# Four quadrants of TensorE in a chunked recurrence, and an attention product moved one stage earlier

## What is computed

```
merged = sigmoid(g_attn) * (attn @ w_branch_attn) + sigmoid(g_ssm) * (ssm @ w_branch_ssm)
x = x + merged @ w_out
```

```
def step(s, inp):
    r_t, w_t, k_t, v_t, a_t, b_t = inp
    sa = jnp.einsum('bhvk,bhk->bhv', s, a_t)
    s = s * w_t[:, :, None, :] + sa[..., :, None] * b_t[:, :, None, :] + v_t[..., :, None] * k_t[:, :, None, :]
    return s, jnp.einsum('bhvk,bhk->bhv', s, r_t)
```

## Time and profile before

| | us |
|---|---|
| median of three runs | 3174.82 |
| the profiled execution, its own time | 3175.19 |
| its span, first to last instruction | 3173.4 |
| the state space stage, 471 to 592 us of the span | 121 |
| merge, 630 to 946 us | 316 |
| the chunk recurrence's body, 1604 to 2163 us | 559 |

### The profile page before, as it was taken

The page is one execution under the profiler, slowest core; times in us unless marked ns, Lnnn a source line. Parts: engine busy times, 40 slices in busy tenths (PEclk is TensorE's granted clock), DMA queues, the critical chain, the costliest instruction groups (busy, mean ns, idle before and its releaser), DMA issues. The chain is left out here.

```text
span 3173.4 us, 62863 instructions
## 1 busy us (share of the span) xinstructions
PE 2646.6 (83%) x26974; PEld 2124.9 (67%) x26974; DVE 1730.7 (55%) x2178; ACT 945.1 (30%) x1392; POOL 638.7 (20%) x618
## 2 busy tenths in 40 slices
PE   4798985689989379997879999995495489999993
PEld 1586644456657368885279999993275478888882
DVE  2791549411114422664645555555533679999993
ACT  2121431200003310001323222321102057777772
POOL 0221458021100023220064434430000011001000
PEclk8899997889999689997589999997695579999997
DMA  9231003111113211110411111001325069999994
GB/s 372 68 142 66 1 15 104 45 43 40 53 36 130 91 53 60 47 41 11 159 36 24 24 24 24 17 11 44 139 93 207 0 265 403 399 399 395 394 388 148
DMA packets 128123, 397.55 MB, mean 125 GB/s; under 512 B 54570, under 2 KB 64426, under 8 KB 98066
## 3 DMA queue, kind: packets, MB, share of 16 engines
q1 hardware_dynamic: 116948, 355.32, 29.9%
q0 software_dynamic: 4608, 16.78, 2.2%
q10 hardware_dynamic: 6336, 21.99, 1.8%
HBM read 342.64 MB, written 51.42 MB: 124 GB/s over the span
## 5 line engine op out<-in xcount | busy, mean ns | idle before, releaser
L2832 DVE TENSOR_TENSOR ex_wl<-ew_raw,ex_wh 128x2048 fp32r<-128x2048 f32 x192 | 435.6, 2290 | 42.0 <-ACT ex_wh L2794 38.5
L2794 ACT ACTIVATE ex_wh<-ew_raw 128x2048 fp32r<-128x2048 f32 x192 | 367.5, 1919 | 216.1 <-PEq L89 109.3
L125 PE MATMUL sp_acc<-b2h_hi,sp_wh 128*128 128x512 f32 (+1 forms) x528 | 194.5, 368 | 12.0 <-POOL sp_wl L1534 12.0
L125 PE MATMUL sp_acc<-b2h_lo,sp_wh 128*128 128x512 f32 (+1 forms) x528 | 194.4, 368 | 0.0
L125 PE MATMUL sp_acc<-b2h_hi,sp_wl 128*128 128x512 f32 (+1 forms) x528 | 194.1, 368 | 0.0
L1022 DVE TENSOR_TENSOR merge_sg<-merge_acc,merge_sg 128x512 f32<-128x512 f32 x32 | 20.6, 686 | 264.3 <-ACT merge_sg L1008 264.3
L2073 ACT ACTIVATE rc_xt<-rc_ps 128x256 f32<-128x256 f32 x160 | 61.3, 383 | 243.9 <-PE rc_ps L2214 243.9
L2214 PE MATMUL rc_ps<-rc_x,rc_lm 64*64 64x64 f32 x3200 | 129.5, 219 | 2.3 <-DVE rc_x L2147 1.3
L2715 POOL DMA_INDIRECT x<-ex_o,ex_at x16 | 26.5, 1655 | 490.9 <-DVE ex_o L2855 490.9
L125 PE MATMUL merge_acc<-merge_hh,merge_wh 128*128 128x512 f32 x256 | 101.7, 397 | 24.9 <-DVE merge_hl L1015 19.5
L2703 POOL DMA_INDIRECT ex_xs<-h,ex_at x16 | 27.5, 1719 | 457.3 <-DVE ex_at L2857 434.4
(11 more groups left out here) (453 smaller groups left out, 6936.3 us busy)
## 6 DMA issues: line engine op xcount, KB each, us to landing
ew_raw<-in_exp_gate SPq DMA_DIRECT2D x64, 1024.0 KB, 7.2
ew_raw<-in_exp_up SPq DMA_DIRECT2D x64, 1024.0 KB, 9.2
ew_raw<-in_exp_down SPq DMA_DIRECT2D x64, 1024.0 KB, 7.8
b_pj<-in_ada_w SPq DMA_DIRECT2D x24, 1024.0 KB, 18.9
rc_ac<-ac SPq DMA_DIRECT2D x40, 256.0 KB, 3.7
merge_w<-in_w_merge SPq DMA_DIRECT2D x16, 512.0 KB
ac<-rp_ac SPq DMA_DIRECT2D x4, 2048.0 KB, 7.2
pr_w<-in_w_main SPq DMA_DIRECT2D x14, 512.0 KB
```

Of the source, the lines that this page charges most:

```text
L125: ins = nc.tensor.matmul(out, w[a][:, k, :], h[b][:, k, cols], start=(first and n == 0), stop=(last and n == 2))
L2794: nc.scalar.activation(wh[:, n % RING], raw[:, n % RING], ACT.Copy).then_inc(q["w_hi"], 1)
L2832: V.tensor_tensor(wl[:, n % RING], raw[:, n % RING], wh[:, n % RING].bitcast(f32), ALU.subtract).then_inc(q["w_lo"], 1)
```

## The change

Three edits. (1) In the recurrence both directions share PSUM: `ps[n]` has two banks, and the bank is chosen by the rows of the array that a product uses. `crossing` issues four products at a time, one for each quadrant, two of each direction; a head's result may then lie on the other half of the partitions (heads are paired, `paired`), since transposes now take whole 128 x 128 blocks (two heads of both halves; `turned`) and move a matrix to the other half as well. Products that must stay on their half (`staying`: with the state `S`, and the inverse) use two quadrants as before, into a bank chosen by direction. The parts of `right_side`, `outputs` that use the state are separate blocks, evacuated separately (`gs`, and a second addition to `y`); `solved` then has two terms. VectorE no longer makes the first transposed start value: it is transposed by TensorE and copied by ScalarE like at the other levels. One semaphore for both directions is waited for where there were two. The order of the steps is somewhat changed. (2) In `s5`, 16 units of the attention product (8 blocks x 2 halves, four k each) stand between the other work of TensorE; ScalarE copies each (`pF`, one bank) and stores it to DRAM (`branch`). `inputs` is cut into halves of one bank. (3) `merge` loads `branch` back into `merged` ahead of everything else, issues the state space product alone, and weighs the attention branch from `merged`.

State space stage (new parts):

```diff
-        pU = ph.ps("pU", [P, 2, 512])
+        pU = ph.ps("pU", [P, 512])
+        pF = ph.ps("pF", [P, 512])
+        out = pj[:, 6, :].rearrange("p (s n) -> p s n", s=2)
+        wb = pj[:, 7, :].rearrange("p (s k n) -> p s k n", s=2, k=4)
 # scalar
+                def branches(*units):
+                    for u in units:
+                        act.wait_ge(q["b_summed"], u + 1)
+                        if u >= 2:
+                            act.wait_ge(stored[u % 2], 16 * (u // 2))
+                        nc.scalar.activation(out[:, u % 2], pF[:], ACT.Copy).then_inc(q["b_ready"], 1)
+                        act.wait_ge(q["b_ready"], u + 1)
+                        act.dma_start(branch[u // 2, :, (u % 2) * 512:(u % 2 + 1) * 512], out[:, u % 2]).then_inc(stored[u % 2], 16)
 # tensor
+                def branches(*units):
+                    for u in units:
+                        b, h = u // 2, u % 2
+                        if h == 0:
+                            pe.wait_ge(b_loaded[b % 2], 16 * (b // 2) + 16)
+                        if u:
+                            pe.wait_ge(q["b_ready"], u)
+                        for k in range(4):
+                            last = nc.tensor.matmul(pF[:], wb[:, b % 2, k, :], pj[:, PJ_ZA + k, h * 512:(h + 1) * 512], start=(k == 0), stop=(k == 3))
+                        last.then_inc(q["b_summed"], 1)
 # tensor, order
-                inputs(0)
+                inputs(0, 0)
+                inputs(0, 1)
                 chunk_sums(0)
-                inputs(1)
+                inputs(1, 0)
+                branches(0)
+                inputs(1, 1)
+                branches(1)
                 chunk_sums(1)
-                for a in range(PASSES):
+                branches(2, 3)
+                for a in range(2):
                     outputs(a)
-                    if a + 2 < PASSES:
-                        inputs(a + 2)
+                    inputs(a + 2, 0)
+                    branches(4 * a + 4)
+                    inputs(a + 2, 1)
                     back(a)
-                    if a + 2 < PASSES:
-                        chunk_sums(a + 2)
+                    chunk_sums(a + 2)
+                    branches(4 * a + 5, 4 * a + 6, 4 * a + 7)
+                outputs(2)
+                back(2)
+                branches(12, 13, 14, 15)
+                outputs(3)
+                back(3)
```

Merge:

```diff
             def _(sp):
+                for b in range(KD):
+                    sp.dma_start(merged[:, b, :], branch[b]).then_inc(a_loaded, 16)
                 with sp.Fori(0, KD) as b:
...
-                        for r, first in enumerate((PJ_ZA, PJ_ZS)):
-                            for k in range(4):
-                                last = nc.tensor.matmul(acc[:, 4 * h + 2 + r, :], wb[:, 4 * r + k, :], pj[:, first + k, hs], start=(k == 0), stop=(k == 3))
+                        for k in range(4):
+                            last = nc.tensor.matmul(acc[:, 4 * h + 2, :], wb[:, k, :], pj[:, PJ_ZS + k, hs], start=(k == 0), stop=(k == 3))
...
+                dve.wait_ge(a_loaded, 16 * KD)
                 dve.sem_inc(done, 2)
...
-                        for r in range(2):
-                            nc.vector.tensor_tensor(sg[:, h, r, :], acc[:, 4 * h + 2 + r, :], sg[:, h, r, :], ALU.mult).then_inc(weighed, 1)
+                        nc.vector.tensor_tensor(sg[:, h, 0:1, :], merged[:, ds(b, 1), h * 512:(h + 1) * 512], sg[:, h, 0:1, :], ALU.mult).then_inc(weighed, 1)
+                        nc.vector.tensor_tensor(sg[:, h, 1, :], acc[:, 4 * h + 2, :], sg[:, h, 1, :], ALU.mult).then_inc(weighed, 1)
```

Recurrence, TensorE's new helpers and body (waits left out where a line of dots stands):

```diff
+        ps = [ph.ps(f"ps{n}", [P, 2, 512]) for n in range(4)]
-            b["ps"] = [ph.ps(f"ps{d}{i}", [P, 512]) for i in range(4)]
+        def crossed(n, d, w=CK):
+            return ps[n][:, :, d * 2 * w:(d + 1) * 2 * w].rearrange("p f (j t) -> p j f t", t=w)
+        def stayed(n, d, half=0):
+            return ps[n][:, d, half * HP * CK:(half + 1) * HP * CK].rearrange("p (h t) -> p h t", t=CK)
-                def heads(out, l, r, start=True, stop=True):
-                    for e in range(2):
-                        c = slice(e * CK, (e + 1) * CK)
-                        last = M(out[c], l[c], r[c], start=start, stop=stop)
+                def crossing(n, w, *terms):
+                    for j, s in product(range(HP // 2), range(2)):
+                        for i, (l, r) in enumerate(terms):
+                            for d, c in product(range(2), range(2)):
+                                f = c ^ s ^ d
+                                k, h, at = slice(f * CK, (f + 1) * CK), 2 * j + c, (2 * d + j) * w
+                                last = M(ps[n][c * CK:(c + 1) * CK, f, at:at + w], l(t[d])[k, h], r(t[d])[k, h], start=(i == 0), stop=(i == len(terms) - 1))
+                def staying(n, half, l, r):
+                    for h, d, c in product(range(HP), range(2), range(2)):
+                        k = slice(c * CK, (c + 1) * CK)
+                        last = M(stayed(n, d, half)[k, h], l(t[d])[k, h], r(t[d])[k, h], start=True, stop=True)
+                def turned(out, m):
+                    for j in range(HP // 2):
+                        pair = slice(2 * j, 2 * j + 2)
+                        last = nc.tensor.transpose(out[:, pair].rearrange("p h t -> p (h t)"), m[:, pair].rearrange("p h t -> p (h t)"), T.ident[:])
...
+                def body(i, sl, old, following):
                     products(i, 0, sl)
                     if old is not None:
                         right_side(i, 1 - sl)
+                    x_turned(i, 0, sl)
+                    crossing(3, 2 * CK, (lambda b: b["kst"][:, sl], lambda b: b["ar"][:, sl])).then_inc(joint["pk_done"], 1)
+                    if old is not None:
+                        right_side_of_state(i, 1 - sl)
                     advanced(i, 0, sl)
                     products(i, 1, sl)
+                    x_turned(i, 1, sl)
                     if old is not None:
                         solved(i, 1 - sl)
                     advanced(i, 1, sl)
...
+                            last = turned(stayed(3, d, half_), b[n][:, sl])
...
                     products(i, 2, sl)
+                    x_turned(i, 2, sl)
                     if old == "all":
                         outputs(i, 1 - sl)
                     advanced(i, 2, sl)
+                    if old == "all":
+                        outputs_of_state(i - CTX_CK, 1 - sl)
+                    products(i, 3, sl)
+                    x_turned(i, 3, sl)
                     if old is not None:
+                        state(i, 1 - sl)
+                    advanced(i, 3, sl)
+                    products(i, 4, sl)
+                    x_turned(i, 4, sl)
                     if following:
...
                         lower(i + 1, 1 - sl)
...
+                    for d in range(2):
+                        turned(stayed(3, d), t[d]["vst"]).then_inc(q[d]["v_done"], 1)
+                    advanced(i, 4, sl)
                     if following:
                         lower_rows(i + 1, 1 - sl)
-                    advanced(i, 4, sl)
```

More of the change, by code:

```diff
@@ L672, in _, with s5 @@
                         gate(it - 3)
-def s5(nc, T, uc, I, yT, work, rot, kept):
+def s5(nc, T, uc, I, yT, pj, rot, kept, branch):
     DG = 2 * GP
@@ L731, in _, with weights @@
                         sp.dma_start(wi[s * GC:(s + 1) * GC, :, :, :], kept.taps[a, :, :, CT - 1 - s:2 * CT - 1 - s, :]).then_inc(q["c_loaded"], 16)
+                def weights(b):
+                    if b >= 2:
+                        sp.wait_ge(q["b_summed"], 2 * b - 2)
+                    sp.dma_start(wb[:, b % 2], I["w_merge"][b, :, 2 * KD:2 * KD + 4]).then_inc(b_loaded[b % 2], 16)
+                sums(0)
+                weights(0)
+                weights(1)
+                outputs(0)
+                sums(1)
+                weights(2)
+                sums(2)
+                weights(3)
+                outputs(1)
+                sums(3)
+                weights(4)
+                weights(5)
+                outputs(2)
+                weights(6)
+                weights(7)
+                outputs(3)
             @block.gpsimd
@@ L1914, in rwkv_chunks @@
                 b[n] = ph.sb(f"{n}{d}", [P, 2, HP, CK])
-            for n in ("e_neg", "tmp", "t1", "vst", "v", "g", "u", "sum", "S"):
+            for n in ("e_neg", "tmp", "t1", "vst", "v", "g", "gs", "u", "sum", "S"):
                 b[n] = ph.sb(f"{n}{d}", [P, HP, CK])
@@ L2113, in masked @@
                         b, s = t[d], q[d]
-                        dve.wait_ge(s["t1_done"], LEVELS * i + l + 1)
-                        V.tensor_tensor(b["t1"][:], small(b["ps"][0]), over(T.level[d][l + 1][:]), ALU.mult).then_inc(s["t1_ready"], 1)
+                        dve.wait_ge(joint["t1_done"], LEVELS * i + l + 1)
+                        V.tensor_tensor(paired(b["t1"][:]), crossed(0, d), over(T.level[d][l + 1][:]), ALU.mult).then_inc(s["t1_ready"], 1)
```

(28 more changed lines are left out.)

295 lines of the change are left out of this document (131 added, 164 removed).

## The result

| | before | after |
|---|---|---|
| median of the runs | 3174.9 us | 3128.02 us (3126.26 to 3131.54) |
| ratio, 95% interval | | 0.9856 (0.9839 to 0.9873) |
| profiled execution: span | 3173.4 us | 3127.7 us |

The changed kernel is 47 us faster. I had forecast 139 us, and 3128 lies outside my range (2995 to 3100). The sign was right, the size was not.

The account below looks back on a forecast made before the run. Recurrence and merge were taken as bound by TensorE's stream of products, the state space stage not. 3175.2 - 105 (recurrence) - 48.5 (merge) + 14 (state space) = 3036 us; range 2995 to 3100.

Parts of the forecast that it names:

- the stage is explained by slots alone: Recurrence before the change: record slots sum to 27.8 us per full chunk, against 559 / 20 = 28.0.
- The sum for the changed chunk, 22.3 us: Recurrence: 17.2 us of TensorE work plus 4.6 idle, 21.5 in the first five chunks, plus 0.5 allowance.
- 0.5 for all of it: Recurrence: 0.5 us added per chunk for operations running beside GpSimd and for waits on two semaphores.
- bare schedule of 21.8: Recurrence: full chunk of 17.2 us TensorE work and 4.6 us idle, before the 0.5 allowance.
- The unknown prices: Recurrence: VectorE reading two banks, taken as nothing (possibly +40 us); four operands per slot instead of two, no row available.
- A: Recurrence: quadrants share no slot beyond pairs; 304 slots added, +9.6 us per chunk, stage +80, total 3221; chance 0.07.
- B: Recurrence: least spacing of 25 ns for every record, +5.7 us per chunk, stage 568, total 3150; chance 0.10.
- C: Recurrence: the clock falls, half the stage at 1.2 GHz, +8.6 us per chunk, total 3208; chance 0.04.
- the new stalls are at most 1.8 us: Recurrence, under the clock rival: TensorE's new idle pauses last no longer than 1.8 us each.
- 416 x 0.058 + 32 x 0.109: Recurrence before: narrow and wide pairs of a full chunk times their slot lengths, given as 27.8 us.
- forecast +3.5: Merge: branch loads queued ahead of the first weights delay TensorE's start by 3 to 5 us, taken as +3.5.
- The wait on `done`: Merge: state space half products end before the sum does, costing 0.4 us seven times, +3 in all.

Follow-up runs that it names:

- warm: The changed kernel with 96 more records (three crossings into a bank nobody reads) in TensorE's pause before each chunk: 3134.25 us, ratio 0.9866.
- two_at_a_time: The changed kernel with a crossing's outermost loop over s and f = c ^ s, 16 records in a row on the same two quadrants: 3177.16 us.
- late_turn: The changed kernel with GpSimd's factors held until x's start value, and x's transpose blocks replaced by crossings with the identity: 3176.94 us, ratio 1.0003.
- two_quadrants: The changed kernel with the loop over directions outermost in a crossing, the alternation of f kept: 3127.77 us, ratio 0.9846.

## Why the prediction was right and wrong

**The step that failed** is the claim that "the stage is explained by slots alone", carried over to a stage whose slots are half as long. It was true of the kernel before. The sum for the changed chunk, 22.3 us, has TensorE's slots and its waits for VectorE, and no term for how fast instructions arrive. Measured: 27.5. Of the 5.2 us missing, the stalls are 2.3. The additions beside GpSimd are 0.8 (2 x 0.83 less 2 x 0.42); I had seen that GpSimd lengthens VectorE's operations and put 0.5 for all of it. That 0.5 is already in the 22.3, so against the bare schedule of 21.8 the gap is 5.7. The half clock behind the longer pause is 1 to 1.5, which is an estimate: 0.45 for the transposes, 0.9 for the wide block and some for the block ahead, in most chunks; the run warm, at a clock of 1.00, is 1.6 us shorter outside its stalls. Between half a microsecond and one remains, which I leave open.

**The slots themselves were right.** Taking for every block the shortest time that it and the pause behind it have in 13 chunks, the sum for a chunk of the changed kernel is 23.2 us, or 22.4 without the 0.8 of the slow additions; my schedule says 21.8, and 22.3 with the allowance. A crossing takes 0.47 us, transposes 0.58 to the next block, the pauses behind levels 0 and 3 are 0.95 and 0.98 (forecast 1.16 and 1.31). Once GpSimd is out of the way, the pause ahead of a chunk is 1.62 us where 1.83 was forecast.

**The unknown prices.** Reading two banks costs VectorE nothing: 419 ns. Four operands instead of two per slot cost nothing: 32 records in 0.69 us.

**The rivals.** A is refuted by that row, and the quadrants' worth is shown by two_at_a_time: 29.4 us less stalls against 25.2. B, a least spacing of 25 ns for every record, is refuted too: records of a crossing start 14.6 ns apart. C was half right. The clock did fall, to 0.93, but not by half of the stage, and it cost 1 to 1.5 us per chunk where I had priced 8.6. It also needed a cause that I had excluded ("the new stalls are at most 1.8 us"). My own sign of being wrong, a clock below 0.95 in the recurrence, came. No rival had the instruction supply. The chance should have gone there, since the profile of before had the row: 92 instruction loads in 366 us, one per 4 us, for an engine whose records I was about to issue at twice the pace inside the crossings.

Three slips in the sums change nothing in this account: 416 x 0.058 + 32 x 0.109 is 27.6, not 27.8; rival A's 9.6 us goes with 272 slots, not 304; and its +80 leaves out the tail of 8 us, with which A would be some 7 us later.

**State space and merge.** The outputs of the four passes were forecast at 508.5, 539.2, 568.3 and 594.6 us; the stage began 1.4 us later than before, and they start as follows:

```profile
509.71 1.19 PE L890 MATMUL s_pB<-s_wi,s_um 128*128 128x128 f32 x4 [6.41 <-DVE s_x L964]
...
540.96 0.61 PE L890 MATMUL s_pB<-s_wi,s_um 128*128 128x128 f32 x4
...
569.69 0.61 PE L890 MATMUL s_pB<-s_wi,s_um 128*128 128x128 f32 x4
...
595.37 0.61 PE L890 MATMUL s_pB<-s_wi,s_um 128*128 128x128 f32 x4
```

That part holds step by step, the 3.43 us of a unit and the 1.1 us for its copy included. In merge TensorE starts 18.8 us into the stage where it was 16.1 before: +2.7 (forecast +3.5), and the row names the split weights as I had it:

```profile
664.50 0.79 PE L125 MATMUL merge_acc<-merge_hh,merge_wh 128*128 128x512 f32 x1 [21.69 <-POOL merge_wl L119]
```

The branch loads' starts lie 29.7 us apart (695.62, 725.32), before 36.6 (685.63, 722.25): 6.9 less, the full eight records twice over. The wait on `done`, for which I had set 0.4 us seven times, costs nothing. With the 0.8 us of the earlier start this is 3.8 of the 4.5 us by which merge was better.

## What to carry to other kernels

Instruction supply is a limit like any other: before and after an edit, work out how long the densest run of 256 instructions lasts. The mean over a stretch is not enough: before, 64 instructions per us lost next to nothing, and after, 60 (outside the stalls) lost 2.3 us per chunk. Here loads of 256 were hidden where a block lasted 3.7 us or more, and came late in dense runs, where it would last 1.9 us and the load took some 2.4. When an edit makes products shorter rather than fewer, look for forms with fewer instructions (whole-block transposes, one term instead of two), and don't fill pauses with products. When a stage is shortened, ask what now runs beside the operations on its path: GpSimd's loop had been harmless until the chunk's end came to lie beside it.

## What I had not expected of the hardware

- Where TensorE stood waiting for a block of 256 instructions (16 KB), the block's first matmul came 2.2 to 2.9 us after its load began (median 2.4). At two quadrants' pace little is lost (0.15 us per chunk before, 0.5 in two_at_a_time); at four, single stalls of up to 1.5 us, and up to 3.0 in late_turn.
- 285 instructions more per chunk, in the place of 20 whole-block transposes that take TensorE longer, cost 3.7 us per chunk in stalls.
- VectorE's addition with both operands in SBUF takes 0.83 us (up to 0.98) where a GpSimd operation is already running and 0.42 alone; with one operand in PSUM it stays at 0.42.
- TensorE takes up 64 x 64 products on free quadrants past ones that wait for theirs: in two_at_a_time the next block's products started (1905.89) while the block before still had some to start (1905.94). The order of issue within a crossing made no difference in two_quadrants, where all four quadrants come up within a few products.
- Replacing the transposes of `x` by products did not raise the clock (0.98 to 0.95). The Trainium skill (TensorE: Matmul & The Clock Gate, "Part 4: PE-mode transpose") says that a transpose does not count as busy in the same way as a product. No run here shows that: warm kept its 32 transposes per chunk at a clock of 1.00, and in late_turn the longer stalls can hide such an effect, so this stays open.

Open too is what decides when the next block is asked for: the loads' starts lie mostly 50 to 115 records ahead of the boundary, and no run here varied that alone.
